# Expert rows gathered by index and results scattered by GpSimd, through a table of choices by slot, in a hybrid decoder layer

## What is computed

```python
comb = jnp.sum(jax.nn.one_hot(top_i, EXPERTS_PER_GROUP, dtype=jnp.float32) * top_p[..., None], axis=1)
...
for g in range(N_EXPERT_GROUPS):
    sl = slice(g * EXPERTS_PER_GROUP, (g + 1) * EXPERTS_PER_GROUP)
    hid = jax.nn.silu(jnp.einsum('md,edf->mef', x, w_gate[sl])) * jnp.einsum('md,edf->mef', x, w_up[sl])
    wg = jnp.where((g_sel == g)[:, None], comb, 0.0).astype(x.dtype)
    y = y + jnp.einsum('mef,me,efd->md', hid, wg, w_down[sl])
```

## Time and profile before

| | us |
|---|---|
| median of 3 executions | 990.02 (989.5 to 995.6) |
| the profiled execution | 990.65 |
| its span | 988.8 |
| TensorE busy | 840.3 (85%) |
| VectorE busy | 476.0 (48%) |
| ScalarE busy | 262.2 (27%) |
| GpSimd busy | 171.9 (17%) |
| moved by the DMA engines | 207.43 MB, mean 210 GB/s |
| mean granted TensorE clock | 0.925 of full speed |

### The profile page before, as it was taken

The page is one execution under the profiler, slowest core; times in us unless marked ns, Lnnn a source line. Parts: engine busy times, 40 slices in busy tenths (PEclk is TensorE's granted clock), DMA queues, the critical chain, the costliest instruction groups (busy, mean ns, idle before and its releaser), DMA issues.

```text
span 988.8 us, 12301 instructions
## 1 busy us (share of the span) xinstructions
PE 840.3 (85%) x4729; PEld 595.2 (60%) x4729; DVE 476.0 (48%) x1076; ACT 262.2 (27%) x648; POOL 171.9 (17%) x141
## 2 busy tenths in 40 slices
PE   5999798999988888999999899869899976866910
PEld 5998788988877875888888344555533322312300
DVE  5997476666568577873353144370121111101158
ACT  4221443434263256563321011100011100000100
POOL 2673534342015340100000000021000000000030
PEclk9999899999979788999999999969999989978965
DMA  8321354543071124842512760429999999999252
GB/s 302 90 82 33 128 198 156 223 148 129 2 274 51 54 82 144 302 172 74 214 77 85 321 274 1 170 91 399 361 424 424 425 430 401 426 402 423 122 195 85
DMA packets 38667, 207.43 MB, mean 210 GB/s; under 512 B 9053, under 2 KB 9661, under 8 KB 28049
## 3 DMA queue, kind: packets, MB, share of 16 engines
q1 hardware_dynamic: 29056, 172.28, 45.0%
q0 software_dynamic: 5136, 18.36, 5.2%
q10 hardware_dynamic: 4416, 15.99, 4.0%
HBM read 168.48 MB, written 38.05 MB: 209 GB/s over the span
## 4 chain that ended last, share of the span: by engine, by line
PE 47%; issue 31%; DVE 17%; DMA 2%; POOL 2%; ACT 1%; SPq 1%; POOLq 0%; DVEq 0%; ACTq 0%
PE bank L581 9%; PE bank L582 9%; PE bank L583 9%; PE bank L574 8%; DVE r_f L1468 6%; PE bank L765 2%; PE bank L797 1%; PE bank L671 1%; DMA x_f<-in_conv_state 1%; PE bank L705 1%; POOL scr_x L2148 1%; PE bank L796 1%; PE bank L801 1%; PE bank L683 1%; DVE r_f L1825 1%
## 5 line engine op out<-in xcount | busy, mean ns | idle before, releaser
L989 PE MATMUL bank<-x_f,r_f 128*64 128x512 f32 x272 | 126.9, 622 | 16.3 <-ACT r_f L1365 8.5
L581 PE MATMUL bank<-r_r,w_r 128*128 128x268 f32 x416 | 125.8, 302 | 10.9 <-DVE w_r L1445 10.3
L582 PE MATMUL bank<-y_r,w_r 128*128 128x268 f32 x416 | 122.1, 293 | 0.0
L583 PE MATMUL bank<-r_r,w_r 128*128 128x268 f32 x416 | 121.9, 293 | 0.0
L582 PE MATMUL bank<-w_r,r_r 128*128 128x512 f32 x240 | 96.3, 401 | 0.0
L581 PEld LDWEIGHTS bank<-r_r,w_r 128*128 128x128 f32 x416 | 82.1, 197 | 15.8 <-DVE w_r L1445 10.3
L581 PE MATMUL bank<-x_r,r_r 128*128 128x512 f32 x200 | 81.8, 409 | 3.9 <-DVE w_r L1752 3.8
L582 PEld LDWEIGHTS bank<-y_r,w_r 128*128 128x128 f32 x416 | 81.8, 197 | 0.0
L583 PEld LDWEIGHTS bank<-r_r,w_r 128*128 128x128 f32 x416 | 81.6, 196 | 0.0
L583 PE MATMUL bank<-x_r,w_r 128*128 128x512 f32 x200 | 80.4, 402 | 0.0
L989 PEld LDWEIGHTS bank<-x_f,r_f 128*64 128x64 f32 x272 | 38.3, 144 | 69.4 <-issue 68.1
(11 more groups left out here) (345 smaller groups left out, 1604.8 us busy)
## 6 DMA issues: line engine op xcount, KB each, us to landing
x_f<-in_w_gu SPq DMA_DIRECT2D x17, 2048.0 KB, 29.3
w_f<-in_w_d SPq DMA_DIRECT2D x22, 1024.0 KB, 29.9
y_f<-in_w_gu SPq DMA_DIRECT2D x10, 2048.0 KB, 27.5
w_f<-in_w_f SPq DMA_DIRECT2D x26, 512.0 KB, 4.3
scr_x<-y_f SPq DMA_DIRECT2D x25, 512.0 KB, 6.1
w_f<-in_w_gu SPq DMA_DIRECT2D x6, 2048.0 KB, 21.5
x_f<-in_w_d SPq DMA_DIRECT2D x11, 1024.0 KB, 31.5
w_f<-in_w_t SPq DMA_DIRECT2D x5, 2048.0 KB, 8.2
```

Source lines behind the costliest of these rows:

```text
L581: pe.matmul(out, ah, bh, start=start, stop=False)
L582: pe.matmul(out, ah, bl, start=False, stop=False)
L583: return pe.matmul(out, al, bh, start=False, stop=stop)
L989: ins = pe.matmul(out[half, :], XT[:, k, half], wgu[s][:, k, :], start=(k == 0), stop=(k == KC - 1))
```

## The change

- `h1` is stored in the order of the tokens, each row twice (rows 2n and 2n + 1 of `scr_h`), by ScalarE behind each tile of the mix stage: ten plain stores.
- VectorE works out for each choice its number `token_at` (2 times the token, plus 0 or 1) and where it stands in the table (`at_id`). GpSimd scatters these numbers, four bytes each, into a table in HBM that was filled with an index beyond the last row, and reads it back as `rows_at`: for each slot the choice that sits in it.
- GpSimd gathers each pair's X from `scr_h` by `rows_at` and scatters its Y to `scr_y` by the same numbers. An index beyond the bound leaves the row out. X[1] is set to zero once; what is not gathered stays what it was.
- In the overflow loop GpSimd reads a column of the table before each gather and each scatter.
- The result is then in the order of the tokens, so the last stage reads it with ten plain loads on SyncE.
- The zero stores, ScalarE's loads of X and its stores of Y go.
- Two semaphores are merged into others (`sconv_dv` into `conv_dv`, `ssilu_ac` into `silu_ac`), with no instruction moved.

```diff
+        slot, half_no = more(2 * NT, dtype=I32), more(2 * NT, dtype=I32)
+        twice = more(1)
...
-        slot = small[:, 106:116].bitcast(I32)
-        zeros = Y[:, NT - 1, :]
+        at_id = small[:, 106:116].bitcast(I32)
+        none = Y[0:CAP, NT - 1, 0:CAP].bitcast(I32)
+        rows_at, token_at = cut(RX + 17040, NHALF).bitcast(I32), cut(RX + 17088, 2 * NT).bitcast(I32)
+        bound_at = small[:, 142:144].bitcast(I32)
+        extra_at = [cut(RX + 17098 + i, 1).bitcast(I32) for i in range(2)]
...
-        scr_x = nc.dram_tensor("scr_x", (NRES + P, D), F32).ap()
-        scr_y = nc.dram_tensor("scr_y", (NHALF * CAP, D), F32).ap()
+        scr_h = nc.dram_tensor("scr_h", (2 * NTOKENS, D), F32).ap()
+        scr_y = nc.dram_tensor("scr_y", (2 * NTOKENS, D), F32).ap()
+        scr_id = nc.dram_tensor("scr_id", (CAP * CAP, 1), I32).ap()
+        ids = scr_id.rearrange("(r e) o -> r (e o)", e=CAP)
+        id_column = scr_id.rearrange("(r e) o -> e r o", e=CAP)
+        tokens_h, tokens_y = (a.rearrange("(n k) d -> k n d", k=2) for a in (scr_h, scr_y))
...
-                if i >= FT - N_ZERO:
-                    sp_zeros(sp, i - (FT - N_ZERO))
...
+            stores = 16 * len([b for b in range(NPAIR) if b % 2])
+            all_stored = sp.snap(sp_extras[0] * 16 + stores)
+            sp.wait_ge(S["yw_out0"], 16 * (NPAIR // 2))
+            sp.wait_ge(S["yw_out1"], all_stored)
+            for t in range(NT):
+                r, (a, b) = tile_rows(t), row_cols(t)
+                for k in range(2):
+                    sp.dma_start(G[k][0:r, t, :], tokens_y[k, a:b]).then_inc(S[f"gt{t}"], 16)
...
+                act.wait_ge(S["lnb_dv"], t + 1)
+                a, b = row_cols(t)
+                for k in range(2):
+                    act.dma_start(tokens_h[k, a:b], h1[0:tile_rows(t), t, :]).then_inc(S["h1_out"], 16)
...
-                    if b > 1 and b + 3 < FIRST or b == FIRST:
-                        load_x(act, b + 3 if b < FIRST else FIRST + 2)
-                    if b == FIRST - 3:
-                        act.dma_start(X[1][0:CAP, :], scr_x[NE * CAP:(NE + 1) * CAP, :]).then_inc(S["ex_in"], 16)
-                    if b == FIRST - 2:
-                        load_x(act, FIRST)
...
-                act.wait_ge(S["y_ev"], 2 * (b + 1))
-                at = P * pair_at(b)
-                act.dma_start(scr_y[at:at + P, :], Yout[b % 2]).then_inc(S[f"yw_out{b % 2}"], 16)
...
-                if b == 1:
-                    act.wait_ge(S["sc_out"], 16 * 2 * NT)
-                    load_x(act, N_HOT)
-                    load_x(act, N_HOT + 1)
...
-                act.dma_start(X[1][0:CAP, :].rearrange("p (b d) -> p b d", b=1),
-                              scr_x[NE * CAP:].rearrange("(b p) d -> b p d", p=CAP)[bass.ds(j + 1, 1)].rearrange("b p d -> p b d"))\
-                   .then_inc(S["ex_in"], 16)
...
-                act.wait_ge(S["ex_ac"], j * 3 + 3)
-                act.wait_ge(S["ex_dv"], j * 4 + 4)
-                act.dma_start(scr_y[NE * CAP:].rearrange("(b p) d -> b p d", p=CAP)[bass.ds(j, 1)].rearrange("b p d -> p b d"),
-                              Yout[1][0:CAP, :].rearrange("p (b d) -> p b d", b=1)).then_inc(S["yw_out1"], 16)
...
-            act.wait_ge(S["ex_in"], extras * 16 + 16)
-            at = P * pair_at(FIRST + 1)
-            act.dma_start(X[1], scr_x[at:at + P, :]).then_inc(S["ex_in"], 16)
...
+            link(v.tensor_scalar(twice, pk("iota_p"), 2.0, None, ALU.mult))
+            v.tensor_copy(token_at[:, 0:1], twice)
+            link(v.tensor_scalar(twice, twice, 2.0 * (NSAMP - P), None, ALU.add))
+            link(v.scalar_tensor_tensor(token_at[:, 1:NT], pk("iota32")[:, 1:NT], 2.0 * P, twice.broadcast_to((P, NT - 1)),
+                                        ALU.mult, ALU.add))
+            v.tensor_scalar(token_at[:, NT:2 * NT], token_at[:, 0:NT], 1.0, None, ALU.add)
...
-            v.tensor_tensor(slot, far, base, ALU.add).then_inc(S["rt_dv"], 1)
+            link(v.tensor_tensor(slot, far, base, ALU.add))
+            v.tensor_scalar(half_no, slot, 6, None, ALU.logical_shift_right)
+            link(v.tensor_scalar(at_id, slot, CAP - 1, 6, ALU.bitwise_and, ALU.logical_shift_left))
+            v.tensor_tensor(at_id, at_id, half_no, ALU.bitwise_or).then_inc(S["rt_dv"], 1)
...
-                    v.wait_ge(S["sc_out"], 16 * 2 * NT)
+                    v.wait_ge(S["h1_out"], 16 * 2 * NT)
...
-            p.memset(zeros, 0.0).then_inc(S["zero_pl"], 1)
+            p.memset(none, 2 * NTOKENS).then_inc(S["none_pl"], 1)
+            p.wait_ge(S["none_pl"], 1)
+            p.dma_start(ids, none).then_inc(S["id_out"], 16)
...
-        def pool_scatter(p):
+        def pool_route(p):
+            p.wait_ge(S["lnb_dv"], 1)
+            for i in range(2):
+                p.memset(bound_at[:, i:i + 1], 2 * NTOKENS - 2 - i)
+            p.memset(X[1], 0.0).then_inc(S["none_pl"], 1)
             p.wait_ge(S["rt_dv"], 3)
-            p.wait_ge(S["lnb_dv"], NT)
-            p.wait_ge(S["zero_out"], ZEROED)
+            p.wait_ge(S["id_out"], 16)
             for k in range(2):
                 for t in range(NT):
                     r, c = tile_rows(t), k * NT + t
-                    p.indirect_dma_start(scr_x, bass.IndirectOffsetOnAxis(ap=slot[0:r, c:c + 1].bitcast(U32), axis=0),
-                                         h1[0:r, t, :], None).then_inc(S["sc_out"], 16)
-        def pool_final(p):
-            p.wait_ge(S["moe_ac"], 1)
-            for t in range(NT):
-                for k in range(2):
-                    r, c = tile_rows(t), k * NT + t
-                    p.indirect_dma_start(G[k][0:r, t, :], None, scr_y,
-                                         bass.IndirectOffsetOnAxis(ap=slot[0:r, c:c + 1].bitcast(U32), axis=0))\
-                     .then_inc(S[f"gt{t}"], 16)
+                    p.indirect_dma_start(scr_id, bass.IndirectOffsetOnAxis(ap=at_id[0:r, c:c + 1].bitcast(U32), axis=0),
+                                         token_at[0:r, c:c + 1], None).then_inc(S["id_out"], 16)
+            p.wait_ge(S["id_out"], 16 + 16 * 2 * NT)
+            for u in range(2):
+                p.dma_start(rows_at[CAP * u:CAP * (u + 1), :], ids[:, u:u + NHALF]).then_inc(S["tb_in"], 16)
+            p.wait_ge(S["tb_in"], 32)
...
+        def pool_experts(p):
+            last = 2 * NTOKENS - 1
+            def gather(x, at, done, bound=last):
+                p.indirect_dma_start(x, None, scr_h, bass.IndirectOffsetOnAxis(ap=at.bitcast(U32), axis=0),
+                                     bounds_check=bound, oob_is_err=False).then_inc(S[done], 16)
+            def scatter(at, y, done, bound=last):
+                p.indirect_dma_start(scr_y, bass.IndirectOffsetOnAxis(ap=at.bitcast(U32), axis=0), y, None,
+                                     bounds_check=bound, oob_is_err=False).then_inc(S[done], 16)
+            def gather_pair(b, done):
+                gather(X[x_buffer(b)], rows_at[:, 2 * pair_at(b):2 * pair_at(b) + 1], done)
+            def scatter_pair(b):
+                p.wait_ge(S["y_ev"], 2 * (b + 1))
+                scatter(rows_at[:, 2 * pair_at(b):2 * pair_at(b) + 1], Yout[b % 2], f"yw_out{b % 2}")
+            p.wait_ge(S["h1_out"], 16 * 2 * NT)
+            p.wait_ge(S["none_pl"], 2)
+            gather_pair(N_HOT, f"xs_in{x_buffer(N_HOT)}")
+            for b in range(FIRST):
+                if b:
+                    p.wait_ge(S["xtr_mm"], min(b + 2, FIRST))
+                    if b + 3 <= FIRST and b != FIRST - 3:
+                        gather_pair(b + 3, f"xs_in{x_buffer(b + 3)}")
+                    elif b == FIRST - 3:
+                        gather(X[1][0:CAP, :], rows_at[0:CAP, NE:NE + 1], "ex_in")
+                    elif b == FIRST - 2:
+                        gather_pair(FIRST, f"xs_in{x_buffer(FIRST)}")
+                scatter_pair(b)
+            extras = p.value_load(table[0:1, 0:1], min_val=1, max_val=NOV)
+            before = 16 * len(range(1, FIRST, 2))
+            bounds = [p.value_load(bound_at[0:1, i:i + 1], min_val=1, max_val=last) for i in range(2)]
+            with p.Fori(0, extras) as j:
+                p.wait_ge(S["ex_mm"], j * 4 + 1)
+                p.dma_start(extra_at[0][0:CAP, :].rearrange("p (e o) -> p e o", e=1),
+                            id_column[bass.ds(j + (NE + 1), 1)].rearrange("e r o -> r e o"),
+                            allow_slow_non_contiguous=True).then_inc(S["tb_in"], 16)
+                p.wait_ge(S["tb_in"], j * 32 + 48)
+                gather(X[1][0:CAP, :], extra_at[0][0:CAP, :], "ex_in", p.snap(bounds[0] + 1))
+                p.wait_ge(S["yw_out1"], j * 16 + before)
+                p.dma_start(extra_at[1][0:CAP, :].rearrange("p (e o) -> p e o", e=1),
+                            id_column[bass.ds(j + NE, 1)].rearrange("e r o -> r e o"),
+                            allow_slow_non_contiguous=True).then_inc(S["tb_in"], 16)
+                p.wait_ge(S["tb_in"], j * 32 + 64)
```

(10 more changed lines are left out.)

46 lines of the change are left out of this document (16 added, 30 removed).

## The result

The changed kernel takes 978.47 us in the median (975.69 to 983.75, 4 runs) beside 990.51 us of the kernel before (989.5 to 995.6, 4 runs): a ratio of 0.9885, 95% interval 0.9849 to 0.9921. A repetition gave 980.41 us (979.74 to 980.78, 5 runs) beside 990.55, ratio 0.9895, interval 0.9878 to 0.9912. So 10 to 12 us are gained; 979.3 us was forecast. The profiled execution is the slowest of the four: 983.75 us, span 981.9.

The account below looks back on a forecast made before the run. Weight and row bytes through the DMA engines were taken to bound the kernel up to pair 12. Terms: -11.5 + 0.5 + 1.0 - 0.7 = -10.7 us, from 990.0 to 979.3 us; range 972 to 986, overall 971 to 993.

Parts of the forecast that it names:

- Pair 12's start: Pair 12's gate-up, set by the weight stream, would start 11.5 us earlier, at about 844.6 us.
- The rows: Leaving out empty X and Y rows takes 6.16 MB from the stream before pair 12: -14.7 us at 420 GB/s.
- The early X of pairs 3 and 4: Gathered before the saturated stretch, their remaining rows leave it: -1.1 us; +1.3 us charged for a hole they no longer fill.
- Rows by index at 351 instead of 420 GB/s: Indirect row transfers inside the saturated weight stream run at the slower rate: 4.37 MB cost +2.1 us.
- Route: Five small added VectorE instructions in the route, ahead of the experts, delay it: +0.9 us.
- Zeros: Dropping the zero stores beside the projection's matmuls gains nothing, since no row shows anybody waiting behind them: 0.
- Entry to the loop: Before the overflow loop, pair 12's store passes GpSimd while ScalarE sheds the loop's transfers: +0.5 us, between 0 and 1.3.
- Pair 14's X: Behind the overflow loop, this load is issued later because it stands on GpSimd behind the loop's scatter: +1.0 us.
- Tail: Last output copy to VectorE's last stage: scatter and ordered loads, no gap before the second tile: -0.7 us, -3 to +3.
- Dummies: Rival, chance 0.10: empty rows are not skipped but still move, at 351 GB/s; 995.7 us.
- Drag: Rival, chance 0.10: indirect gathers and scatters slow the whole weight stream to 357 GB/s; 1000.2 us.
- The late chain: Rival, chance 0.15: GpSimd's column read, gather, column read in the overflow loop delay pair 14's X by 5.3 us; 983.6 us.

Follow-up runs that it names:

- full_xy: Changed kernel with empty slots pointed at spare rows, so every gather and scatter moves all its rows; 989.53 us, ratio 0.9997 to the kernel before.
- x3_late: Changed kernel with the gathers of pairs 3 and 4 held back until pair 1's result is complete; 982.2 us, one run, read by its profile.
- plain_12: Changed kernel with pair 12's result first stored plainly by ScalarE, which waits on that before the overflow loop; scatter follows; 984.7 us, one run.
- static_columns: Changed kernel with the overflow loop's two column reads replaced by table columns already in SBUF, store wait kept; 979.03 us.
- zeros_back: Changed kernel with 25 zero stores of 512 KB put back in the projection, into a spare tensor; 978.81 us.

## Why the prediction was right, and where it was so by luck

**The bound.** Right. With all rows back (full_xy) the median is within 0.1% of the kernel before; TensorE still waits 9.8 us for weights in pairs 9 to 12 with rows left out, so bytes bound the stretch yet.

**Pair 12's start, -11.5 us.** Counted from the route's small products it is 209.96 us before and 198.56 after, -11.4. That the sum is right to 0.1 us is luck; the terms under it were off in both directions:
- The rows, -14.7: of it 1.4 us are the empty rows of X3 and X4, which belong to their own term. The other 13.3 measured 10.3. Pair 11's Y doesn't stand ahead of pair 12's weights, and the hole swallows part of what comes early.
- The early X of pairs 3 and 4: -1.4 - 1.1 + 1.3 = -1.2 forecast, -1.9 by the one profile of x3_late.
- Rows by index at 351 instead of 420 GB/s, +2.1: wrong, it is 0. From 740 to 850 us the changed kernel moves 423 GB/s, and the kernel before 421. The 351 of the earlier trace rows was a rate of full engines (a share of 0.96), so that it was lower is no matter of idle time. It isn't the price of the index either: the changed kernel reads the same results with ordered loads in its last stage, and from 944 to 949 us they move 360 GB/s at a share of 0.97 (second row below). The rate belongs to that stage; why it is lower there than in the experts' stage was not tried. This error covered most of the first.
- Route, +0.9: 0.7 at the first pick, 0.4 at the first gate-up.
- Zeros, 0: right for the 25 stores that were put back.

```profile
740.00:850.00 110.00, 96.08 (x452) 35.87 (x450) 17.09 (x32) 12.43 (x24) 15.33 (x16) 0.97 1.01 423
...
944.00:949.00 5.00, 0.00 (x0) 0.00 (x0) 4.86 (x7) 0.20 (x1) 0.00 (x0) 0.50 0.97 360
```

**Entry to the loop, +0.5 (0 to 1.3).** Mis-sized: TensorE's wait ahead of the extra gate-up went from 7.43 to 11.32 us, +3.9, of which pair 13's start shows +2.3, since the products behind it ran 1.3 us shorter (8.77 for 10.09). I priced only the issue, 0.6 us more, and set 0.4 of ScalarE's relief against it, which makes 0.2 and not the 0.5 that I took (plain_12 puts the way through GpSimd at 0.9), and let the landing stand at its old time, 7.9 us, where it was 11.0.

**Pair 14's X, +1.0.** It came out as -0.6 (4.04 us for 4.63). The issue did come later by about what I gave it: GpSimd issues it 6.5 us behind the start of the last down products, ScalarE did 5.8, so +0.7. But the X landed sooner, 11.2 us behind its issue instead of 12.8, and that was no term of mine.

**Tail, -0.7.** -0.4 for the round trip and -0.9 for the gap before the second tile, -1.3 in all.

Behind pair 12 these make +0.8 in the forecast and 0.0 in the profiles (132.7, then 132.6 and 132.8): again a miss of each term, made up by the others.

**The rivals.** Dummies: full_xy is that kernel, at 989.5, against 995.7 forecast; the +5.2 for their slower rate was the same error as above. Drag: none, 417 GB/s with all rows by index. By the Trainium skill, "DMA: Bandwidth & Descriptors", section "Latency and other measured facts", contention around GpSimd-written rings is a best guess for slow engines; no run here shows it. The late chain: its waits are real, 9.69 us for the first column and 8.31 for the second once the store wait is away. My working for it had both column reads at 12.7 us, the time of pair 14's X; they took 9.7 and 8.3. The chain decides nothing in the changed kernel (static_columns). Without the store wait it makes pair 14's wait 4.2 us longer, and taking both columns from SBUF shortens the last piece by 5.7.

**What would show it.** Bytes fell by 25.6 MB rather than "some 21", since the zeros were 17.3 MB and not 13.1; the other 8.3 are close to the 8 that this leaves in my "some 21". Pair 3 waits for no X, as forecast. Pair 12 started at 849.3, outside 842 to 848, for the 4.6 us lost early; in zeros_back and the repetition it is 844.0 and 846.3. Pairs 10 and 11 waited 3.6 and 2.4 us for weights, inside the 2 to 5, pair 12 only 1.0. The engines were full to about 895 us (428 GB/s from 890 on, then 384). From VectorE's first instruction of the last stage to the end it is 37.9 us where it was 39.0: the 36 in the forecast was a little short, the gap of 0.95 is the difference.
